# Sum pieces of the output weights: eight in the merge stage, or four there and four in the next input projections

## The reference

```python
# first block: three branches, gated and merged, then the output weights
branch = einsum('nbsw,nwd->nbsd', ys, w_branch)         # 3 x (512x512 @ 512x1024)
gates  = sigmoid(gate_logits)                           # part of h @ w_in, 3 x 1024 columns
merged = einsum('bsnd,nbsd->bsd', gates, branch)
x      = x + merged @ w_out                             # 512x1024 @ 1024x1024
# second block
proj   = rms_norm(x) @ w_in_2                           # 512x1024 @ 1024x4400
u, q, kc, vc, ksl, vsl, kwn, vwn, g_nsa, g_merge = split(proj)
k_cmp  = gelu(flat(kc + pe_k) @ w_ck1) @ w_ck2          # and v_cmp from vc
...                                                     # pooling, attention
merged = g_a * (y_pool @ w_proj_pool) + g_b * (y_nsa @ w_proj_nsa)
x      = x + merged @ w_out_2
x      = x + square(relu(rms_norm(x) @ w_ff1)) @ w_ff2
return rms_norm(x)
```

## Time and profile before

| | us |
|---|---|
| median of three runs | 1468.23 (1467.72 to 1471.29) |
| the profiled execution's time | 1470.67 |
| its span | 1468.9 |
| PE busy in the span | 1425.5 (97%) |
| DVE busy | 873.8 (59%) |
| ACT busy | 666.4 (45%) |
| POOL busy | 610.3 (42%) |

### The profile page before, as it was taken

How to read it: one execution, slowest core, us unless ns; L and a number is a source line. 1 busy time by engine, 2 the same in 40 slices (tenths; PEclk the granted TensorE clock), 3 DMA queues, 4 the chain that set the end, 5 groups by cost and what they waited for, 6 DMA issues and landing times.

```text
span 1468.9 us, 20996 instructions
## 1 busy us (share of the span) xinstructions
PE 1425.5 (97%) x7693; PEld 1189.1 (81%) x7693; DVE 873.8 (59%) x1646; ACT 666.4 (45%) x1176; POOL 610.3 (42%) x433
## 2 busy tenths in 40 slices
PE   8999999989989998999999999999999999999998
PEld 7888888768778876889998777788888888888886
DVE  4336968456654477560326677773065787777776
ACT  5453645567564333353323566773224433223342
POOL 4333744344343343444443255653425233333330
PEclk9999999999999999999999999999999999999999
DMA  6222433203102789766522110003265433333321
GB/s 205 83 82 83 148 95 90 60 12 93 42 2 58 269 288 339 283 219 210 173 82 81 58 44 1 2 2 132 98 206 196 145 107 108 100 100 100 100 86 58
DMA packets 90651, 170.31 MB, mean 116 GB/s; under 512 B 7031, under 2 KB 31170, under 8 KB 90562
## 3 DMA queue, kind: packets, MB, share of 16 engines
q1 hardware_dynamic: 89282, 165.89, 34.9%
q10 hardware_dynamic: 1280, 3.22, 0.6%
HBM read 148.12 MB, written 20.97 MB: 115 GB/s over the span
## 4 chain that ended last, share of the span: by engine, by line
PE 86%; DMA 5%; DVE 2%; ACT 2%; issue 2%; SPq 1%; POOL 1%; POOLq 0%; DVEq 0%; ACTq 0%
PE bank L1037 53%; PE bank L1723 9%; PE bank L1299 4%; PE bank L1100 4%; PE bank L1307 4%; PE bank L1130 4%; PE bank L966 3%; DMA sums_lo<-chunk_a_lo 2%; DMA sums_lo<-projr 1%; PE bank L997 1%; PE bank L1132 1%; DMA raw<-in_w_in 1%; DMA raw<-in_w_out 1%; SPq L666 1%; PE bank L1711 1%
## 5 line engine op out<-in xcount | busy, mean ns | idle before, releaser
L802 POOL TENSOR_TENSOR w_lo<-raw,w_hi 128x1024 fp32r<-128x1024 f32 (+3 forms) x185 | 433.7, 2354 | 512.7 <-ACT w_hi L1799 512.4
L1799 ACT ACTIVATE w_hi<-raw 128x1024 fp32r<-128x1024 f32 (+3 forms) x189 | 191.3, 1015 | 384.3 <-DMA raw<-in_w_in 190.2
L1037 PE MATMUL bank<-xt_hi,w_hi 128*128 128x512 f32 x560 | 222.9, 398 | 6.6 <-POOL w_lo L802 3.4
L1037 PE MATMUL bank<-xt_hi,w_lo 128*128 128x512 f32 x560 | 219.2, 391 | 0.0
L1037 PE MATMUL bank<-xt_lo,w_hi 128*128 128x512 f32 x560 | 219.1, 391 | 0.0
L1037 PE MATMUL bank<-w_hi,xt_hi 128*128 128x484 f32 (+2 forms) x520 | 192.1, 369 | 0.0
L1037 PE MATMUL bank<-w_lo,xt_hi 128*128 128x484 f32 (+2 forms) x520 | 190.1, 366 | 0.0
L1037 PE MATMUL bank<-w_hi,xt_lo 128*128 128x484 f32 (+2 forms) x520 | 190.1, 366 | 0.0
L1037 PEld LDWEIGHTS bank<-xt_hi,w_hi 128*128 128x128 f32 x560 | 105.8, 189 | 31.7 <-issue 10.4
L1037 PEld LDWEIGHTS bank<-xt_hi,w_lo 128*128 128x128 f32 x560 | 105.7, 189 | 22.7
L1037 PEld LDWEIGHTS bank<-xt_lo,w_hi 128*128 128x128 f32 x560 | 105.9, 189 | 21.7 <-issue 0.5
(11 more groups left out here) (453 smaller groups left out, 2986.4 us busy)
## 6 DMA issues: line engine op xcount, KB each, us to landing
raw<-in_w_in SPq DMA_DIRECT2D x40, 512.0 KB, 3.6
raw<-in_w_in SPq DMA_DIRECT2D x40, 484.0 KB, 3.4
raw<-in_w_ff SPq DMA_DIRECT2D x36, 512.0 KB, 3.6
quarter_b<-in_w_ff SPq DMA_DIRECT2D x28, 512.0 KB, 3.5
raw<-in_w_in SPq DMA_DIRECT2D x24, 392.0 KB, 3.4
w_hi<-sums_hi SPq DMA_DIRECT2D x16, 512.0 KB, 4.7
w_lo<-sums_lo SPq DMA_DIRECT2D x16, 512.0 KB, 5.8
raw<-in_w_branch SPq DMA_DIRECT2D x12, 512.0 KB, 6.2
```

Of the source, the lines that this page charges most:

```text
L802: pool.tensor_tensor(w_lo[:, slot, 0:halves, 0:width], raw[:, slot, 0:halves, 0:width], w_hi[:, slot, 0:halves, 0:width].bitcast(F32), ALU ...
L1037: ins = pe.matmul(o, lhs, rhs, start=st and j == 0, stop=en and j == 2)
L1799: act.activation(w_hi[:, slot, 0:halves, 0:width], raw[:, slot, 0:halves, 0:width], ACT.Copy)\
```

## The change

The pieces are shared out anew. Pieces 0 to 3 (of `w_out`) are made in the merge stage, one for every four pairs: SP loads piece c behind merge pair 8 + 4c and stores it behind pair 11 + 4c, and ACT rounds it behind the `next_hi` of pair 6 + 4c. Pieces 4 to 7 (of `w_out_2`) are made in the next input projections: SP loads them behind input pairs 8, 13, 18 and 23, and stores them behind pairs 12, 17, 22 and behind the fourth pair of the gates. They all use the buffer over `mix2` (`CHUNK_BUFFER`), so a load waits there for the store before it. ACT rounds them behind input pairs 7, 12, 17 and 23. DVE does the work on a piece in one go (`whole_chunk`). The last change is apart from this: in the last `weigh` of each block DVE signals merged rows in pairs as their additions are done (`final=True`), where `merged_lo` had signalled them once for four additions.

```diff
+CHUNK_BUFFER = (0, 1, 0, 1, 0, 0, 0, 0)
...
+def chunk_uses(c):
+
+    return CHUNK_BUFFER[:c + 1].count(CHUNK_BUFFER[c])
...
-                k, kt, w = c % 2, c % 4, (w_out, w_out_2)[c // 4]
+                k, kt, w = CHUNK_BUFFER[c], c % 4, (w_out, w_out_2)[c // 4]
                 if c < 2:
                     sp.wait_ge(sem["emptied_d"], strips_emptied("D", STRIP_MERGE + 3))
+                elif c == 4:
+                    sp.wait_ge(sem["pair_used"], strip_end(STRIP_OUT1 + 1))
                 else:
...
             def side_transfers(j):
 
-                if j >= 7 and j % 2 == 1 and (j - 7) // 2 < 8:
-                    chunk_store((j - 7) // 2)
-                if j >= 4 and j % 2 == 0 and (j - 4) // 2 < 8:
-                    chunk_load((j - 4) // 2)
+                c, place_ = divmod(j - 8, 4)
+                if 0 <= c < 4 and place_ == 0:
+                    chunk_load(c)
+                if 0 <= c < 4 and place_ == 3:
+                    chunk_store(c)
...
+                    if 4 * j + q in (8, 13, 18, 23):
+                        chunk_load(4 + (4 * j + q - 8) // 5)
+                    if 4 * j + q in (12, 17, 22):
+                        chunk_store(4 + (4 * j + q - 12) // 5)
...
-            stream(PAIR_M2, w_in_2[0], GATES2, S, 2)
+            stream(PAIR_M2, w_in_2[0], GATES2, S, 1)
+            chunk_store(7)
+            stream(PAIR_M2 + 4, w_in_2[0], GATES2 + S, S, 1)
...
+            def chunk_high(c):
+
+                act.wait_ge(sem["chunk_summed"], 3 * c + 3)
+                act.activation(chunk[CHUNK_BUFFER[c]][2], chunk[CHUNK_BUFFER[c]][0], ACT.Copy).then_inc(sem["chunk_hi"], 1)
...
                 for j in range(12):
                     next_hi(PAIR_MERGE + 12 * n + j, S)
-                    c, odd = divmod(12 * (n - 1) + j - 5, 2)
-                    if 0 <= c < 8 and not odd:
-                        act.wait_ge(sem["chunk_summed"], 3 * c + 3)
-                        if c >= 2:
-                            act.wait_ge(sem[f"chunk_out{c % 2}"], 64 * (c // 2))
-                        act.activation(chunk[c % 2][2], chunk[c % 2][0], ACT.Copy).then_inc(sem["chunk_hi"], 1)
+                    c, place_ = divmod(12 * (n - 1) + j - 4, 4)
+                    if 0 <= c < 4 and place_ == 2:
+                        chunk_high(c)
                     if j == 7:
@@ ACT, input projections
             for q in range(7, 11):
                 next_hi(I + q, IN2_W)
+                if q == 7:
+                    chunk_high(4)
...
             for q in range(11, 15):
                 next_hi(I + q, IN2_W)
+                if q == 12:
+                    chunk_high(5)
...
             for q in range(16, 19):
                 next_hi(I + q, IN2_W)
+                if q == 17:
+                    chunk_high(6)
...
             hidden_turned()
+            chunk_high(7)
@@ DVE, weigh and merged_lo
+                        if final and m % 2:
+                            ins.then_inc(sem["merged_in"], 1)
+                    if not final:
+                        step(ins)
...
             def merged_lo(c, n, b):
 
-                dve.sem_inc(sem["merged_in"], 1)
@@ DVE, merge stage
+            def whole_chunk(c):
+
+                sum_chunk(c)
+                chunk_lo(c)
...
-                if n == 1:
-                    chunk_work((0, 0), (0, 1))
-                if n == 2:
-                    chunk_work((5, 0), (5, 1), (6, 0), (6, 1))
+                if n:
+                    whole_chunk(0 if n == 1 else 3)
                 for b in range(2 if n else 0):
                     scale_gates1(STRIP_MERGE + 4 * n + b, lambda m: cols(GATED, 4 * b + m))
-                    if n == 1:
-                        chunk_work(*(((3, 0), (3, 1)) if b else ((1, 0), (1, 1), (2, 0), (2, 1))))
-                    elif b == 0:
-                        chunk_work((7, 0), (7, 1))
+                    if n == 1 and b == 0:
+                        whole_chunk(1)
                 for b in range(2):
-                    weigh(STRIP_MERGE + 4 * n + 2 + b, n == 0, GATED if n else None, MERGED)
+                    weigh(STRIP_MERGE + 4 * n + 2 + b, n == 0, GATED if n else None, MERGED, final=n == 2)
                     if n == 1 and b == 0:
-                        chunk_work((4, 0), (4, 1))
+                        whole_chunk(2)
                     if n == 2:
                         merged_lo(MERGED, 0, b)
                         sum_rows(0, b)
@@ DVE, input projections
+            whole_chunk(4)
+            whole_chunk(5)
             for k, (name, pe_col) in enumerate((("ck", VEC["pek"]), ("cv", VEC["pev"]))):
...
+            whole_chunk(6)
             dve.wait_ge(sem["tanh_out"], 1)
...
+            whole_chunk(7)
             for k, name in enumerate(("kcmp", "vcmp")):
...
+            dve.wait_ge(sem["chunk_out0"], 64 * chunk_uses(7))
             scale_gates(0, 0)
```

More of the change, by code:

```diff
@@ L656, in chunk_load @@
                     sp.dma_start(chunk[k][0][:, 2 * half_:2 * half_ + 2, :], w[0, r:r + P, :].rearrange("p (c n) -> p c n", c=2))\
-                      .then_inc(sem[f"chunk_in{k}"], 16)
+                       .then_inc(sem[f"chunk_in{k}"], 16)
             def chunk_store(c):
-                k, kt = c % 2, c % 4
-                for made_, src, dst in (("chunk_hi", chunk[k][2], sums_d[c // 4][0]), ("chunk_lo", chunk[k][1], sums_d[c // 4][1])):
-                    sp.wait_ge(sem[made_], c + 1)
+                k, kt = CHUNK_BUFFER[c], c % 4
+                for made, src, dst in (("chunk_hi", chunk[k][2], sums_d[c // 4][0]), ("chunk_lo", chunk[k][1], sums_d[c // 4][1])):
+                    sp.wait_ge(sem[made], c + 1)
                     for half_ in range(2):
                         r = S * half_ + P * kt
-                        sp.dma_start(dst[r:r + P, :].rearrange("p (c n) -> p c n", c=2), src[:, 2 * half_:2 * half_ + 2, :].bitcast(F32))\
-                          .then_inc(sem[f"chunk_out{k}"], 16)
+                        sp.dma_start(dst[r:r + P, :].rearrange("p (c n) -> p c n", c=2),
+                                      src[:, 2 * half_:2 * half_ + 2, :].bitcast(F32)).then_inc(sem[f"chunk_out{k}"], 16)
             def side_transfers(j):
-                if j >= 7 and j % 2 == 1 and (j - 7) // 2 < 8:
-                    chunk_store((j - 7) // 2)
-                if j >= 4 and j % 2 == 0 and (j - 4) // 2 < 8:
-                    chunk_load((j - 4) // 2)
+                c, place_ = divmod(j - 8, 4)
[3 more added lines that the diff above has]
+                    chunk_store(c)
             def merge_weights(n):
-                j = 12 * (n - 1)
                 for s in range(2):
@@ L697, in out_weights @@
             def out_weights(n, p0, w):
-                for k in range(2):
-                    sp.wait_ge(sem[f"chunk_out{k}"], 64 * (2 * n + 2))
+                for c in (4 * n + 2, 4 * n + 3):
+                    sp.wait_ge(sem[f"chunk_out{CHUNK_BUFFER[c]}"], 64 * chunk_uses(c))
                 for i, m in enumerate(OUT_PRODUCTS):
@@ L2214, in _ @@
             for k in range(2):
[L2215 removed]
+                act.wait_ge(sem[f"chunk_out{k}"], 128)
             act.wait_ge(sem["ys_lo"], 2)
@@ L2897, in cols, with weigh @@
                 return proj[:, m // 2, c + S * (m % 2):c + S * (m % 2) + S]
-            def weigh(strip, first, gated, merged, part=None):
+            def weigh(strip, first, gated, merged, part=None, final=False):
                 b = strip % 2
@@ L3030, in chunk_lo @@
                 dve.wait_ge(sem["chunk_hi"], c + 1)
-                dve.tensor_tensor(chunk[c % 2][1], chunk[c % 2][0], chunk[c % 2][2].bitcast(F32), ALU.subtract)\
+                whole, low, high = chunk[CHUNK_BUFFER[c]]
+                dve.tensor_tensor(low, whole, high.bitcast(F32), ALU.subtract)\
                    .then_inc(sem["chunk_lo"], 1)
-            def chunk_work(*steps_):
-                for c, low in steps_:
-                    if low:
-                        chunk_lo(c)
-                    else:
-                        sum_chunk(c)
+            def whole_chunk(c):
+                sum_chunk(c)
+                chunk_lo(c)
             for n, c in enumerate((YTA, YTB, YTM)):
```

20 lines of the change are left out of this document (8 added, 12 removed).

## The result

The changed kernel takes 1539.76 us (median of 4 runs, 1535.85 to 1541.97), the kernel before 1468.28 in the same comparison. The ratio is 1.048, with an interval of 1.0463 to 1.0492. It is slower by 71.5 us; forecast were 57, in a range of 1491 to 1543. The profiled execution has a span of 1537.2 us, 68.3 more than before.

A forecast was written before the change was run, and what follows sets the result against it. PE, busy 97% of the span, was taken as the bound, so only its waits or clock count. Merge stage +23.9, projections +35.9 and signal -0.9 gave +58.9 us; 1525 us was forecast, range 1491 to 1543.

The forecast's parts named there:

- The waits of the merge stage: Merge stage: PE waits for w_lo at pairs 7, 15, 19, 5.4 us each, and for a bank before pair 10, 11.5 us.
- The clock: Low PE clock behind waits: 6.7 us added in the merge stage, 5.4 us in the input projections.
- I count half of them: Merge stage: half a 2.7 us clock restart behind each of the three 5.4 us waits, 4.0 us together.
- rival D: Whole forecast plus low clock behind all short waits too: 9.4 us more, 1534 to 1545; chance 0.12.
- The pairwise signal: Output products: ACT rounds first merged rows while DVE adds the others, giving back at most PE's 0.9 us wait.
- The projections: Input projections: four PE waits of 3.0, 16.1, 8.6 and 2.8 us plus 5.4 of clock, +35.9 us.
- The wait at pair 8: Input projections: behind piece 4's rounding POOL finishes late, so PE gets pair 8's low part 3.0 us late.
- The sum: Whole kernel: merge stage +23.9, projections +35.9, pairwise signal -0.9, together +58.9 us.
- the likeliest case's own range: Whole kernel: the main forecast, slower, 1505 to 1540 us; chance 0.70.
- The other rule: Piece transfers: fixed part shrinks from about 2 us to 0.2 in lighter load; 11 landings would make the sum 20 us smaller.
- Rival C: Both stages: not slower, pieces early enough, the saved 10.5 and 0.9 us remain, 1457; chance 0.03.
- The prediction's 503 and 701 us: Latest moments for DVE to have piece 0's sum (merge stage) and piece 5's (projections) without delaying PE.

The follow-up runs named there:

- experiments 2 and 3: Changed kernel, merge pieces' rounding and sums placed later by arrival (e2): 1496.59 us; changed kernel, merge pieces' loads issued two pairs earlier instead: 1498.31 us.
- e1: Changed kernel with only DVE's piece 1 moved behind the first weigh, no longer between the two gate strips: 1534.38 us, ratio 1.0441.
- e12: Changed kernel with only DVE's piece 5 moved behind the evictions of ck and cv: 1530.11 us, ratio 1.0421.
- e7: Kernel before with only the pairwise signal of merged rows added: 1469.03 us, ratio 0.9996.
- e5: e6 with ACT's load of the residual moved behind the first two next_hi of the output products: 1461.29 us, ratio 0.9953.
- e6: Changed kernel with merge pieces placed as in e2 and projection pieces placed again, piece 5 ahead of the rotation: 1466.08 us, ratio 0.9984.
- e2: Changed kernel with the merge stage's pieces placed on ACT and DVE by when they arrive, loads and stores unchanged: 1496.59 us, ratio 1.0188.
- experiment 4: The run e12: changed kernel with DVE's piece 5 behind the evictions of ck and cv, 1530.11 us.
- e9: Kernel before with ACT's load of the residual moved behind the first two next_hi of the output products: 1469.09 us, ratio 0.9998.
- e4: Changed kernel with merge pieces placed as in e2 and a first placement of the projections' pieces, piece 5 behind the rotation: 1484.56 us, ratio 1.0102.

## Why the prediction was right, and where it was off

**The waits of the merge stage** came at the pairs named. Forecast 5.4, 11.5, 5.4 and 5.4 us; measured 4.94, 11.74, 7.30 and 7.26. The mechanism is shown from both ends by experiments 2 and 3. The first two are right to half a microsecond, the second partly by luck: piece 1 took 7.4 us to arrive, not 6.46, and DVE's work behind it was 0.5 us shorter than reckoned. The last two were mis-sized by 1.9 us each, because the landing of a piece was taken from the first piece of the stage: 6.46 us. Pieces 0 to 3 took 6.1, 7.4, 8.5 and 8.4 us from issue to DVE's start. Pieces 2 and 3 follow close behind a store:

```profile
559.68 2.76 SPq L674 DMA_DIRECT2D sums_lo<-projr  x2
563.42 0.37 SPq L585 DMA_DIRECT2D raw<-in_w_in  x1
563.84 1.76 SPq L664 DMA_DIRECT2D chunk_a<-in_w_out  x2
...
572.32 0.69 DVE L3044 TENSOR_TENSOR chunk_a<-chunk_a 128x512 f32<-128x512 f32 x1 [22.62 <-DMA chunk_a<-in_w_out]
```

That the store is what made them late is argued from these rows; no run took it away alone.

**The clock.** Forecast were 2.7 us behind the long wait and half of it behind each short one, 6.7 in all. Measured are 1.9 to 2.6 us behind each of the four, 8.9 in all. The step that was off is "I count half of them": the clock fell to 0.50 behind all three short waits too, as rival D had it, though each cost less than the 2.7 us that D gives it. How much a wait costs this way differs between executions. Over the six us behind the wait before pair 7 the clock was 0.73 in the changed kernel (515 to 521), 0.50 in e1 and 0.75 in e12 (516 to 522), with a wait of 4.9 to 5.0 us ahead of each.

**The output products** are where a term had the wrong sign. The pairwise signal was priced at -0.9 us, which is PE's wait for `xt_lo` of 0.88 us "in front of the output products". The row shows it elsewhere: the products begin at 612.85, and the wait stands 12.1 us behind that, at the second half of the merged rows:

```profile
624.96 0.47 PE L1100 MATMUL bank<-w_hi,xt_hi 128*128 128x512 f32 x1 [0.88 <-DVE xt_lo L2935]
```

The signal does take this wait away, in e7 and in the changed kernel. In e7 the time stays the same, since a wait for `w_lo` comes instead. In front of the products ACT came to the rows straight from its second `next_hi`, so the signal could not act there. There the changed kernel has a new wait of 2.53 us, with 1.4 us of low clock behind it, and a second one of 1.32 us 25 us later, so 3.9 us of waits where the kernel before had 0.88. The prediction did not count what ACT's load of the residual waits for. In the kernel before it was issued at 595.91, 16.9 us ahead of the products. In the changed kernel it starts with the first loads of `w_out` at 630.24, and the second `w_out` pair is rounded only at 640.38. e5 against e6 shows that moving this load removes the wait in front. That was shown with the pieces placed, not in the changed kernel itself. The 1.32 us were down to 0.6 in e2, with the load in its old place. The row names DVE there, but POOL ended `w_lo` of the third `w_out` pair at about 670.0, 0.1 us ahead of PE's start, so its cause is open.

**The projections.** Forecast 3.0, 16.1, 8.6 and 2.8 us of waits; measured 3.40, 14.59, 8.19 and 0.62. The largest is DVE's order, as forecast: DVE began piece 5 at 749.87 and emptied `cv` at 762.98, where PE went on at 763.08 (experiment 4).

```profile
749.87 0.69 DVE L3044 TENSOR_TENSOR chunk_a<-chunk_a 128x512 f32<-128x512 f32 x1 [23.89 <-DMA chunk_a<-in_w_out]
...
759.97 3.01 DVE L3101 TENSOR_TENSOR flat_v<-bank,vec 64x248 f32<-64x248 f32 x8
```

Two points are off. The wait at pair 8 was to be for `w_lo`; it was for a bank, since ACT's emptying of strip 1 stood behind piece 4 too. The size was right and the releaser was not, which is luck. And piece 7 cost 0.6 us instead of 2.8. The clock took 7.4 us, by subtraction, instead of 5.4: it fell behind the wait of 3.40 us too (0.56 over 728 to 734 us), where none was counted. So the stage came to 34.2 against 35.9.

**The sum** in the span was 68.3 against 58.9. Merge stage and output products make up +10.4 of the difference (3.5 waits, 3.9 at the output products, the other 3.0 clock, by subtraction), the projections -1.7, and 0.7 lies elsewhere. The time of 1539.76 lies at the top of the likeliest case's own range (1505 to 1540) and inside rival D's (1534 to 1545). D's own sum, 58.9 + 9.4 = 68.3, is even what the span shows, but that is luck. Of the 9.4 us of clock that D adds, about 4.2 came, 2.2 in the merge stage and 2.0 in the projections. The rest is made of the longer waits at pairs 15 and 19 and of those at the output products, less what the projections' waits came out shorter.

**The rules weighed.** The row of 3.51 us for `w_lo` beside DVE's subtraction repeats the 3.57 of before. By the Trainium skill ("SBUF — State Buffer", section "Who interferes with whom") two inputs in SBUF on DVE hold up a GpSimd instruction that reads SBUF, and with it the trace agrees again. The other rule was that a transfer's fixed cost shrinks with lighter load (the Trainium skill, "DMA: Bandwidth & Descriptors", section "Latency and other measured facts"), by which the sum would have been 20 us smaller. The DMA share over 470 to 640 us did fall, from 0.81 to 0.46, but pieces 0 to 3 took 6.1 to 8.5 us, and pieces 4 to 7 in the projections took 7.0, 5.3, 6.0 and 5.1. The mean of all eight is 6.7, against 6.46. The four in the projections are 0.6 us faster in the mean. A gain of 1.8 us for each landing is not in the trace. The window, first of the kernel before, then of the changed one:

```profile
470.00:640.00 170.00, 162.28 (x696) 0.98 0.81 285
```

```profile
470.00:640.00 170.00, 138.76 (x574) 0.90 0.46 158
```

**A rival that was refuted on the way.** Rival C's point, that the stage can be rid of its 10.5 us, is true of the idea and not of this version of it. The stage did give 10 us back in e2. The prediction's 503 and 701 us as the latest moments hold for the orders in the diff. With other orders the same loads are early enough.

## What to carry to other kernels

Work fitted between a critical engine's feeders has to be placed from three times, not from one pattern: when its data arrives (issue, plus landing in that traffic, plus the step before), when the in-order engine has the next critical instruction due, and when the store's issuer comes to it. Here the same eight pieces cost 71 us as first placed and gained 2 in e6, or 7 with the residual's load moved (e5). A long wait can hide a second fault that stands in the same place, so count what is gained from a removed wait only after computing the next one. An edit that is worth nothing in one kernel (the residual's load, e9) can be worth 4.8 us in another once the waits around it have gone.

## What the runs showed of the hardware that was not expected

The clock behind a wait of the same length was not the same. At the start of the output products PE stands 2.5 to 2.8 us in eight kernels. In six of them it then ran at 0.50 for about 3 us, in the changed kernel (2.53 us) from the first matmul on, in e2 (2.53 us) from the third. In e4 (2.52 us) and e12 (2.48 us) the clock stayed at full speed. The windows (us, PE busy, clock, DMA share, GB/s) are those of the changed kernel, e12, e2 and e4:

```profile
645.00:650.00 5.00, 4.88 (x16) 0.70 0.43 163
```

```profile
645.00:650.00 5.00, 3.98 (x18) 1.00 0.57 206
```

```profile
605.00:610.00 5.00, 5.00 (x17) 0.66 0.28 103
```

```profile
605.00:610.00 5.00, 4.53 (x20) 1.00 0.53 185
```

Whether PE had stood in the stage before does not decide it. In the changed kernel and in e12 PE had stood four times since the stage's start, in e2 and in e4 it had run without a break, and each pair has one case of either kind. A wait of 3.23 us had the low clock behind it in the kernel before (at 566.53) and full clock in e9 (at 564.03). The waits of 1.2 to 1.65 us in these traces all left the clock at 1.00, and those of 4.9 us and more were all followed by 0.50. What decides between them is open. So what the clock will cost behind one single wait could not be told from these rows.
